# Last steps of a down-projection taken bank by bank, one weight cast with a narrower wait, the last bank in two halves, and a new order of the final normalisation

## The chip, the cores and the metric

The kernel runs on one core of one Trainium2 chip. The metric is device time in microseconds, the median over runs; the kernel before takes 1745.13 us (three runs, 1744.98 to 1745.54).

## What is computed

One decoder layer over 256 tokens with 2048 features, in float32. The part that matters here is its last block, a gated feed-forward layer with a residual and a normalisation behind it:

```python
h = rmsnorm(x, g_pre_ffn[l])
up = causal_dwconv(h @ w_up[l], w_fconv[l], b_fconv[l])
gate, val = jnp.split(up, 2, axis=-1)
x = x + rmsnorm((jax.nn.gelu(gate, approximate=True) * val) @ w_down[l], g_post_ffn[l])
```

`w_up` is 2048 x 11264 and `w_down` 5632 x 2048. `rmsnorm(y, g)` is `y * rsqrt(mean(y*y) + 1e-6) * g` over the 2048 features of a token.

## The kernel before

**Split products.** Each float32 factor is held as a high part (rounded for the matrix unit, type fp32r) and a low part (what the rounding left). A product takes three matmuls, high x high, low x high and high x low (`TERMS`, `rows_mm`, line 540 for its matmul).

**Weight pieces.** All weights come as pieces of up to 1 MB through four slots. For each piece SyncE's queue loads `raw[slot]` once `lo_done` says that the slot's former piece is split (`piece`, L359); ScalarE rounds it into `wsp[slot, 0]` (`hi`, the cast, L1004, semaphore `hi_done`); VectorE subtracts for the low part (`lo`, L1437, `lo_done`); TensorE waits with `arrive` for `lo_done`. A cast may overwrite a slot only when TensorE is done with the piece in it. TensorE counts `gemm_step` for that, and a `Phase` says how many steps a piece is behind: `ph.g(i, 0)` is the count at which trip i begins, `ph.used[c]` the steps of a trip after which piece c is no longer needed. The cast is issued two pieces ahead (`LEAD`), so in a trip of four pieces `hi` is called with c = 2, 3 (the slots 2 and 3 of this trip) and 4, 5 (slots 0 and 1 of the next). For c = 4, 5 it waits for that slot alone; for c = 2, 3 it waits for `ph.g(i, 0)`, that is for all four pieces of the trip before.

**Feed-forward.** The 44 hidden blocks of 128 features go in three groups of 16, 16 and 12 (`GROUPS`). In each, the up-projection (`up_round`) makes the hidden rows in `hsp`, and then the down-projection adds them up in all eight PSUM banks `ps`: bank 4m + b holds tokens 128m to 128m + 127 and output columns 512b to 512b + 511. One weight piece is one hidden block k: 12 matmuls of 512 columns for m = 1, 12 for m = 0, each 3 to a bank. A trip is four blocks; the groups have 4, 4 and 3 trips. The last trip of a group goes in another order (lines 962 to 982): first m = 0 for its four blocks k, all four banks for each; then m = 1. In the groups 0 and 1, m = 1 is also taken block by block; in group 2 bank by bank, with 12 matmuls to a bank. `dn_done` counts finished banks. VectorE takes the sums to `y_tok` (`dn_y`, L2011 copies in group 0, L2013 adds in the others, semaphore `y_out`), the banks of m = 0 before it splits the next two pieces.

On ScalarE the casts of the down-projection of the groups 0 and 1 stand in a hardware loop over all trips, where the trip number i is a register; in group 2 the last trip is written out apart (`last_apart`), with i a Python number:

```python
rounds(act, dn, dn_round, last_apart=(n == len(GROUPS) - 1))
```

**The end.** After the last split VectorE runs, for each half m of the tokens: `dn_y` for four banks, `gain` (y times the gain row, L2031), `fin_rms` (sum of squares from ScalarE, L2037 to L2038, the square root on ScalarE, L991, and a Newton step of five small operations, L1458 to L1462) and `fin` (scale and residual, L2045). Their order is written out: all `dn_y(0, b)`, all `gain(0, b)`, `fin_rms(0)`, then `dn_y(1, b)`, `fin(0, b)`, `gain(1, b)` for each b, `fin_rms(1)`, and four `fin(1, b)`. ScalarE squares each bank with a running sum (L1421). SyncE loads the gain row into `raw` slot 2 after the last split (L453) and stores each finished quarter of 512 columns, 256 KB (L458).

Of the kernel before, what the change touches and what calls it, by code (L numbers as in the profile page):

```python
# [27 lines left out]
ALU = mybir.AluOpType  # L28
ACT = mybir.ActivationFunctionType
AX = mybir.AxisListType.X  # L30
# [127 lines left out]
def build(nc, a, out):  # L158
# [13 lines left out]
    with ExitStack() as ctx:  # L172
# [3 lines left out]
        def sem(name):  # L176
            return ctx.enter_context(nc.semaphore(name))
# [26 lines left out]
        x3_tok, y_tok = a_tok, b_tok  # L204
        g_row, sq_junk = raw[:, 2, :], raw[:, 3, :]
        yg = scr[:, :].rearrange("p (m d) -> p m d", m=2)

# [69 lines left out]
        dn_done, y_out, g_in = sem("dn_done"), sem("y_out"), sem("g_in")  # L277
        fin_sq, fin_out = sem("fin_sq"), sem("fin_out")

# [72 lines left out]
        def _(sp):  # L352
# [100 lines left out]
            sp.dma_start(g_row, a["g_post_ffn"].to_broadcast([P, D])).then_inc(g_in, 16)  # L453
            for m in range(2):
                for b in range(4):
                    sp.wait_ge(fin_out, 4 * m + b + 1)
                    cols = slice(b * 512, (b + 1) * 512)
                    sp.dma_start(out_tok[:, m, cols], out_sb[:, m, cols]).then_inc(out_stored, 16)  # L458
            sp.wait_ge(out_stored, 128)


        @block.tensor
        def _(pe):
# [454 lines left out]
            for n, ((f0, fn), up, dn) in enumerate(zip(GROUPS, PH_UP, PH_DN)):  # L918
# [43 lines left out]
                i, last_ks = dn.trips - 1, range(fn - 4, fn)  # L962
                for c, k in enumerate(last_ks):
                    arrive(dn, i, c)
                    pe.wait_ge(hid_lo, f0 + k + 1)
                    for b in range(4):
                        mm = dn_mm(c, k, 0, b, False, c == 3)
                        if c == 3:
                            mm.then_inc(dn_done, 1)
                if n < len(GROUPS) - 1:  # L970
                    for c, k in enumerate(last_ks):
                        for b in range(4):
                            mm = dn_mm(c, k, 1, b, False, c == 3)
                            if c == 3 and b < 3:
                                mm.then_inc(dn_done, 1)
                        mm.then_inc(gemm_step, 1)
                else:
                    for b in range(4):
                        for c, k in enumerate(last_ks):
                            mm = dn_mm(c, k, 1, b, False, c == 3)  # L980
                        mm.then_inc(dn_done, 1)


        @block.scalar
        def _(act):
# [7 lines left out]
            def hi(ph, i, c):  # L993
# [4 lines left out]
                if c >= SLOTS and c - SLOTS < ph.n:  # L998
                    act.wait_ge(gemm_step, ph.g(i, ph.used[c - SLOTS]))
                elif not isinstance(i, int) or ph.g(i, 0) > 0:  # L1000
                    act.wait_ge(gemm_step, ph.g(i, 0))
# [415 lines left out]
            act.wait_ge(lo_done, PIECES)  # L1417
            for m in range(2):
                for b in range(4):
                    act.wait_ge(y_out, 8 * (len(GROUPS) - 1) + 4 * m + b + 1)  # L1420
                    act.activation(sq_junk[:, b * 512:(b + 1) * 512], y_tok[:, m, b * 512:(b + 1) * 512], ACT.Square,  # L1421
                                   accum_out=st[:, 40 + 4 * m + b:41 + 4 * m + b]).then_inc(fin_sq, 1)
                root(9 + m, st[:, 4 + m:5 + m], st[:, 2 + m:3 + m])


        @block.vector
        def _(dve):
# [598 lines left out]

            def gain(m, b):

                cols = slice(b * 512, (b + 1) * 512)
                dve.wait_ge(y_out, 8 * (len(GROUPS) - 1) + 4 * m + b + 1)  # L2030
                own.mark(dve.tensor_tensor(yg[:, m, cols], y_tok[:, m, cols], g_row[:, cols], ALU.mult))  # L2031

            def fin_rms(m):

                v, root_, r0, r = (st[:, at + m:at + m + 1] for at in (2, 4, 6, 26))
                dve.wait_ge(fin_sq, 4 * m + 4)
                own.link(dve.tensor_reduce(st[:, 48 + m:49 + m], st[:, 40 + 4 * m:44 + 4 * m], AX, ALU.add))  # L2037
                dve.tensor_scalar(v, st[:, 48 + m:49 + m], 1.0 / D, EPS, ALU.mult, ALU.add).then_inc(var_ready, 1)  # L2038
                dve.wait_ge(root_ready, 9 + m)
                newton(v, root_, r0, r)  # L2040

            def fin(m, b):

                cols = slice(b * 512, (b + 1) * 512)
                dve.scalar_tensor_tensor(out=out_sb[:, m, cols], in0=yg[:, m, cols], scalar=st[:, 26 + m:27 + m],  # L2045
                                         in1=x3_tok[:, m, cols], op0=ALU.mult, op1=ALU.add).then_inc(fin_out, 1)
            dve.wait_ge(lo_done, PIECES)
            for b in range(4):
                dn_y(0, b)
            dve.wait_ge(g_in, 16)  # L2050
            for b in range(4):
                gain(0, b)
            fin_rms(0)
            own.wait()
            for b in range(4):
                dn_y(1, b)
                fin(0, b)
                gain(1, b)
            fin_rms(1)
            own.wait()  # L2060
            for b in range(4):
                fin(1, b)

# [107 lines left out]
```

## Time and profile before

| | |
|---|---|
| median of three runs | 1745.13 us |
| the profiled execution's own time | 1745.46 us |
| its span, first to last instruction | 1743.6 us |
| TensorE busy, share of the span | 1727.1 us, 99% |
| VectorE, ScalarE, GpSimd busy | 1141.3, 913.1, 157.1 us |
| mean granted TensorE clock | 0.997 |

The profiled execution lies 1.86 us above its span (launch and end, outside the first and last instruction) and 0.33 us above the median of the runs. Times in the rows further down are microseconds from the span's start; PE is TensorE, PEld its weight loads, DVE VectorE, ACT ScalarE, SPq the issue of transfers by SyncE. A matmul's busy time overlaps the next one's start, so a rate is read from the starts: the stretch between two starts divided by the number of matmuls.

### The profile page before, as it was taken

To read this page: it belongs to the slowest core of one execution; us is meant where nothing else is said; L and a number is where in the kernel's file an instruction comes from. 1 tells how busy PE (TensorE), PEld (TensorE's weight loads), DVE (VectorE), ACT (ScalarE), POOL (GpSimd) and SP (SyncE) were. 2 spreads that over 40 slices of the span, in tenths; PEclk is the share of its full clock that TensorE was granted. 3 is DMA by queue.
4 is the path that set the end of the run, shared out by engine and by line. 5 is a ranking of instruction groups with operands and counts; after the bars stand their busy time and mean duration, and the time that the engine had idled before them with its cause. 6 is when DMAs were issued, how large, how long until landed. Compare 5 with 4: busy or idle time off the path is not lost.

```text
span 1743.6 us, 25292 instructions
## 1 busy us (share of the span) xinstructions
PE 1727.1 (99%) x8956; PEld 1472.3 (84%) x8956; DVE 1141.3 (65%) x1433; ACT 913.1 (52%) x1160; POOL 157.1 (9%) x182
## 2 busy tenths in 40 slices
PE   8999999999999999999999999999999999999997
PEld 7888888888888888888888888888888888888886
DVE  6766675467788874446567677775467776467765
ACT  6656654454567763344447565554345555245542
POOL 0012210000244430000000000000000000000000
PEclk9999999999999999999999999999999999999999
DMA  9544457566555665555654455556465556545552
GB/s 328 191 128 151 155 179 249 193 241 193 171 184 165 196 218 193 193 193 199 235 193 170 145 173 182 180 188 236 150 193 187 181 182 235 180 152 185 192 221 93
DMA packets 214091, 330.09 MB, mean 189 GB/s; under 512 B 5904, under 2 KB 161936, under 8 KB 206608
## 3 DMA queue, kind: packets, MB, share of 16 engines
q1 hardware_dynamic: 208400, 318.49, 54.3%
q10 hardware_dynamic: 5632, 10.79, 1.8%
q8 instruction: 40, 0.66, 0.2%
q14 instruction: 19, 0.16, 0.0%
HBM read 327.16 MB, written 2.10 MB: 189 GB/s over the span
## 4 chain that ended last, share of the span: by engine, by line
PE 98%; DVE 1%; DMA 0%; ACT 0%; SPq 0%; issue 0%; DVEq 0%; ACTq 0%
PE ps L492 50%; PE ps L540 40%; PE ps L508 2%; PE ps L602 1%; PE ps L752 1%; PE ps L680 1%; DMA raw<-in_w_in 0%; PE ps L572 0%; PE ps L709 0%; PE ps L685 0%; PE ps L702 0%; DVE wsp L1437 0%; PE ps L710 0%; PE ps L840 0%; PE ps L824 0%; ACT wsp L1004 0%
## 5 line engine op out<-in xcount | busy, mean ns | idle before, releaser
L1437 DVE TENSOR_TENSOR wsp<-raw,wsp 128x2048 fp32r<-128x2048 f32 (+2 forms) x306 | 676.5, 2230 | 339.7 <-ACT wsp L1004 336.4
L1004 ACT ACTIVATE wsp<-raw 128x2048 fp32r<-128x2048 f32 (+2 forms) x306 | 559.9, 1850 | 297.5 <-PE ps L540 282.2
L492 PE MATMUL ps<-asp,wsp 128*128 128x512 f32 (+1 forms) x3072 | 543.5, 339 | 2.1 <-DVE big_a L1445 1.4
L492 PEld LDWEIGHTS ps<-asp,wsp 128*128 128x128 f32 x3072 | 470.9, 188 | 72.6 <-DVE wsp L1437 1.7
L540 PE MATMUL ps<-wsp,hsp 128*128 128x512 f32 x2304 | 525.7, 389 | 0.0
L540 PEld LDWEIGHTS ps<-wsp,hsp 128*128 128x128 f32 x2304 | 432.1, 188 | 89.5
L492 PE MATMUL ps<-hsp,wsp 128*128 128x256 f32 (+1 forms) x1944 | 353.6, 341 | 3.1 <-DVE hsp L1481 3.1
L492 PEld LDWEIGHTS ps<-hsp,wsp 128*128 128x128 f32 x1944 | 299.9, 189 | 47.2 <-DVE wsp L1437 3.5
L540 PE MATMUL ps<-wsp,asp 128*128 128x512 f32 x768 | 175.5, 389 | 0.0
L1015 ACT ACTIVATE cr<-ps 128x256 f32<-128x256 f32 x185 | 69.0, 379 | 197.7 <-PE ps L492 181.4
L540 PEld LDWEIGHTS ps<-wsp,asp 128*128 128x128 f32 x768 | 143.9, 188 | 29.8
L2133 POOL TENSOR_TENSOR scr<-scr 128x256 f32<-128x256 f32 x44 | 34.1, 795 | 1004.7 <-DVE scr L1963 1004.7
L1378 ACT ACTIVATE scr<-scr,par 128x256 f32<-128x256 f32 x88 | 48.2, 595 | 60.7 <-DVE scr L1952 60.7
L1445 DVE TENSOR_TENSOR cr<-ps,cr 128x256 f32<-128x256 f32 x88 | 35.1, 419 | 44.7 <-ACT cr L1015 44.7
L1957 DVE SCALAR_TENSOR_TENSOR scr<-scr,par 128x255 f32<-128x255 f32 x88 | 42.5, 484 | 27.4 <-ACT scr L1378 27.2
L2114 POOL TENSOR_TENSOR scr<-scr 128x256 f32<-128x256 f32 x16 | 28.5, 1781 | 246.9 <-ACT scr L1190 246.9
L508 PE MATMUL ps<-wsp,asp 128*128 128x512 f32 (+1 forms) x256 | 47.4, 340 | 0.0
L1404 ACT ACTIVATE hsp<-scr 128x256 f32 (+1 forms) x44 | 18.4, 418 | 53.3 <-POOL scr L2133 53.3
L508 PEld LDWEIGHTS ps<-wsp,asp 128*128 128x128 f32 x256 | 40.0, 188 | 5.8
L1992 DVE TENSOR_TENSOR hsp<-scr,hsp 128x256 f32 (+1 forms) x44 | 18.8, 427 | 36.1 <-ACT hsp L1404 36.1
L1109 ACT ACTIVATE scr<-scr,st 128x128 f32<-128x128 f32 (+1 forms) x32 | 14.3, 448 | 49.2 <-DVE st L1615 49.2
L1963 DVE SCALAR_TENSOR_TENSOR scr<-scr,par 128x254 f32<-128x254 f32 x88 | 38.4, 478 | 0.0
(227 smaller groups left out, 910.1 us busy)
## 6 DMA issues: line engine op xcount, KB each, us to landing
raw<-in_w_up SPq DMA_DIRECT2D x88, 1024.0 KB, 5.3
raw<-in_w_in SPq DMA_DIRECT2D x64, 1024.0 KB, 5.4
raw<-in_w_down SPq DMA_DIRECT2D x44, 1024.0 KB, 5.2
raw<-in_w_in SPq DMA_DIRECT2D x32, 768.0 KB, 4.4
raw<-in_w_o_mla SPq DMA_DIRECT2D x16, 1024.0 KB, 5.3
raw<-in_w_o_lru SPq DMA_DIRECT2D x16, 1024.0 KB, 5.1
raw<-in_w_out SPq DMA_DIRECT2D x16, 1024.0 KB, 5.0
raw<-in_w_ukv SPq DMA_DIRECT2D x8, 1024.0 KB, 5.4
```

What stands on the lines that cost most here:

```text
L492: mm = pe.matmul(ps[:, bank, 0:w], lhs(part, k), x[:, 0:w], start=(f and part == 0), stop=(l and n == 1))
L508: mm = pe.matmul(o, x, r, start=(f and part == 0), stop=(l and n == 1))
L540: mm = pe.matmul(ps[:, bank, :], src[:, k, low * T + m * P:low * T + (m + 1) * P], wsp[:, c, part, cols], start=(first and t == 0), stop=( ...
L1004: act.activation(wsp[:, p0 % SLOTS, 0, 0:n], raw[:, p0 % SLOTS, 0:n], ACT.Copy).then_inc(hi_done, 1)
L1015: act.activation(cr[:, slot, :], ps[:, bank, T:2 * T], ACT.Copy, scale=scale).then_inc(cross_done, 1)
L1378: act.activation(UC[2 * v + e], UR[2 * v + e], ACT.Identity, scale=col(W_F + 2 * P, m), bias=col(B_F, m)).then_inc(up_bias, 1)
L1437: dve.tensor_tensor(wsp[:, slot, 1, 0:n], raw[:, slot, 0:n], wsp[:, slot, 0, 0:n].bitcast(F32), ALU.subtract).then_inc(lo_done, 1)
L1445: return dve.tensor_tensor(dst, ps[:, bank, 0:T], cr[:, slot, :], ALU.add)
L1957: own.mark(dve.scalar_tensor_tensor(out=buf[:, 1:T], in0=src[:, 0:T - 1], scalar=col(W_F + P, m), in1=buf[:, 1:T], op0=ALU.mult, op1=ALU.add))
L1963: dve.scalar_tensor_tensor(out=buf[:, 2:T], in0=src[:, 0:T - 2], scalar=col(W_F, m), in1=buf[:, 2:T], op0=ALU.mult, op1=ALU.add).then_inc( ...
L2114: own.mark(pool.tensor_tensor(IG[e], IG[e], XC[e], ALU.mult))
L2133: pool.tensor_tensor(HID[e], UC[e], UC[2 + e], ALU.mult).then_inc(hid_out, 1)
```

## The change

1. In the last trip of **every** group, the m = 0 part now takes its first two blocks as before, and the last two together: for each bank, three matmuls of the third block and three of the fourth. TensorE therefore waits for the fourth piece before the first matmul of the third.
2. `hi` gets a branch: where i is a Python number above 0 and the phase has four pieces a trip, the casts with c = 2, 3 wait for their own slot in the trip before.
3. In group 2, m = 1: banks 0 to 2 as before; the last bank's 12 matmuls of 512 columns become 24 of 256, in two halves. The first half goes on in bank 7; the second starts afresh in bank 0, and VectorE adds both what bank 7 held for these columns and bank 0.
4. The final normalisation is reordered: VectorE waits for the gain row before its first `dn_y`; `dn_y` and `gain` alternate; the finishing operations of m = 0 are spread between the sums of m = 1; the Newton step has three operations in place of five; ScalarE loads its square-root table ahead; the last root takes one addend by `bias`. For m = 1, quarter 0 is finished by TensorE (identity times residual, plus diag(scale) times y*gain, both in plain float32), copied by ScalarE and stored through ScalarE's queue; quarters 1, 2 and the halves of 3 by VectorE and SyncE's queue.

```diff
@@ sync
+            for b in range(4):
+                store(0, quarter(b), b + 1)
+            store(1, quarter(1), 5)
+            store(1, quarter(2), 6)
+            for h in range(2):
+                store(1, LAST[h], 7 + h)
@@ tensor
-                for c, k in enumerate(last_ks):
-                    arrive(dn, i, c)
-                    pe.wait_ge(hid_lo, f0 + k + 1)
+                for cs in ((0,), (1,), (2, 3)):
+                    for c in cs:
+                        arrive(dn, i, c)
+                        pe.wait_ge(hid_lo, f0 + last_ks[c] + 1)
                     for b in range(4):
-                        mm = dn_mm(c, k, 0, b, False, c == 3)
+                        for c in cs:
+                            mm = dn_mm(c, last_ks[c], 0, b, False, c == 3)
...
-                    for b in range(4):
+                    for b in range(3):
                         for c, k in enumerate(last_ks):
                             mm = dn_mm(c, k, 1, b, False, c == 3)
                         mm.then_inc(dn_done, 1)
+                    for h in range(2):
+                        if h:
+                            pe.wait_ge(y_out, 8 * n + 1)
+                        for c, k in enumerate(last_ks):
+                            for t, (part, low) in enumerate(TERMS):
+                                mm = pe.matmul(ps[:, 0 if h else 7, 0:T], hsp[:, k, low * T + P:low * T + 2 * P], wsp[:, c, part, LAST[h]],
+                                               start=(h == 1 and c == 0 and t == 0), stop=(c == 3 and t == 2))
+                        mm.then_inc(dn_done, 1)
+                    pe.wait_ge(y_out, 8 * n + 2)
+                    pe.matmul(ps[:, 1, :], ident[:, :], x3_tok[:, 1, quarter(0)], start=True, stop=False)
+                    pe.wait_ge(y_gain, 1)
+                    pe.wait_ge(fin_diag, 1)
+                    pe.matmul(ps[:, 1, :], diag[0], yg[:, 1, quarter(0)], start=False, stop=True).then_inc(fin_mm, 1)
@@ scalar, hi
                     act.wait_ge(gemm_step, ph.g(i, ph.used[c - SLOTS]))
+                elif isinstance(i, int) and i and ph.n == SLOTS:
+                    act.wait_ge(gemm_step, ph.g(i - 1, ph.used[c]))
                 elif not isinstance(i, int) or ph.g(i, 0) > 0:
                     act.wait_ge(gemm_step, ph.g(i, 0))
@@ scalar, the end
+            act.activation(diag[0], ident[:, :], ACT.Copy, scale=st[:, 27:28]).then_inc(fin_diag, 1)
+            act.wait_ge(fin_mm, 1)
+            act.activation(out_sb[:, 1, quarter(0)], ps[:, 1, :], ACT.Copy).then_inc(fin_first, 1)
+            act.wait_ge(fin_first, 1)
+            act.dma_start(out_tok[:, 1, quarter(0)], out_sb[:, 1, quarter(0)]).then_inc(out_stored, 16)
@@ vector, the end
             dve.wait_ge(lo_done, PIECES)
+            dve.wait_ge(g_in, 16)
             for b in range(4):
                 dn_y(0, b)
-            dve.wait_ge(g_in, 16)
-            for b in range(4):
                 gain(0, b)
...
+            fin(0, quarter(0))
+            dn_y(1, 0)
+            gain(1, 0, y_gain)
+            fin(0, quarter(1))
+            dn_y(1, 1)
+            gain(1, 1)
+            fin(0, quarter(2))
+            fin(0, quarter(3))
+            dn_y(1, 2)
+            gain(1, 2)
```

**TensorE, end of the down-projection of group 1.** A row is an instruction in issue order, xN how many like it follow one another; each pair of a waiting row and an x11 row is one block of m = 0, and the rows shown begin with the third block before, the second block after. Before:

```order
L540 MATMUL ps<-wsp,hsp 128x512 [waits hid_lo,lo_done]
L540 MATMUL ps<-wsp,hsp 128x512 x11
L540 MATMUL ps<-wsp,hsp 128x512 [waits hid_lo,lo_done]
L540 MATMUL ps<-wsp,hsp 128x512 x59
L345 UNCONDITIONAL_BRANCH [waits y_out]
```

After:

```order
L547 MATMUL ps<-wsp,hsp 128x512 [waits hid_lo,lo_done]
L547 MATMUL ps<-wsp,hsp 128x512 x11
L547 MATMUL ps<-wsp,hsp 128x512 [waits lo_done,hid_lo]
L547 MATMUL ps<-wsp,hsp 128x512 x71
L347 UNCONDITIONAL_BRANCH [waits y_out]
```

The wait for the fourth piece has moved up by 12 matmuls, to the head of the third block. The groups 0 and 2 show the same.

**VectorE, from the last two splits on, after the change.** (`big_b` is `y_tok`, `scr` holds y*gain, `raw` the output; before, the first four L2056 stood together and the four L2074 behind them.)

```order
L1480 TENSOR_TENSOR wsp<-raw,wsp 128x2048 [waits hi_done] x2
L2056 TENSOR_TENSOR big_b<-big_b,ps 128x512 [waits dn_done,g_in,lo_done]
L2074 TENSOR_TENSOR scr<-big_b,raw 128x512 [waits y_out]
L2056 TENSOR_TENSOR big_b<-big_b,ps 128x512 [waits dn_done]
L2074 TENSOR_TENSOR scr<-big_b,raw 128x512 [waits y_out]
```

The first sum now waits for the transfer of the gain row, and each `gain` follows the `dn_y` that it needs.

```order
L2088 SCALAR_TENSOR_TENSOR raw<-scr,st,big_a 128x512 x2
L2056 TENSOR_TENSOR big_b<-big_b,ps 128x512 [waits dn_done]
L2074 TENSOR_TENSOR scr<-big_b,raw 128x512 [waits y_out]
L2118 TENSOR_TENSOR big_b<-big_b,ps 128x256 [waits dn_done]
L2119 TENSOR_TENSOR big_b<-big_b,ps 128x256
L2121 TENSOR_REDUCE st<-st 128x1 [waits fin_sq]
L2122 TENSOR_SCALAR st<-st 128x1 [waits dve_self]
L2124 TENSOR_TENSOR big_b<-big_b,ps 128x256 [waits dn_done,dve_self]
```

Two finishing operations of m = 0 (L2088) now stand ahead of the sum of bank 6 and of the last bank; the last bank takes three sums of 256 columns in place of one of 512.

## Rows read from the trace of the kernel before

**Rows 1.** The page: span, busy us, share of it and instruction count by engine.

```profile
span 1743.6 us, 25292 instructions
...
PE 1727.1 (99%) x8956; PEld 1472.3 (84%) x8956; DVE 1141.3 (65%) x1433; ACT 913.1 (52%) x1160; POOL 157.1 (9%) x182
```

**Rows 2.** Who waited for whom on TensorE: total us, times, longest.

```profile
PE ps L492 <- DVE hsp L1481: 3.1, 1, 3.1
...
PE ps L492 <- DVE big_a L1445: 1.4, 1, 1.4
```

**Rows 3.** Timeline of TensorE, group 0's down-projection (start us, length us, instruction, count).

```profile
1179.66 87.21 PE L540 MATMUL ps<-wsp,hsp 128*128 128x512 f32 x384
1266.71 0.50 PE L492 MATMUL ps<-asp,wsp 128*128 128x512 f32 x2
```

**Rows 4.** Timeline of group 0's last trip: casts and splits.

```profile
1245.23 3.72 ACT L1004 ACTIVATE wsp<-raw 128x2048 fp32r<-128x2048 f32 x2 [9.04 <-PE ps L540]
1247.18 4.49 DVE L1437 TENSOR_TENSOR wsp<-raw,wsp 128x2048 fp32r<-128x2048 f32 x2 [8.67 <-ACT wsp L1004]
```

**Rows 5.** Timeline, TensorE, group 1's down-projection.

```profile
1446.86 87.21 PE L540 MATMUL ps<-wsp,hsp 128*128 128x512 f32 x384
1533.91 0.85 PE L492 MATMUL ps<-asp,wsp 128*128 128x512 f32 x4
```

**Rows 6.** Timeline of group 1's last trip: its last two splits.

```profile
1514.38 4.50 DVE L1437 TENSOR_TENSOR wsp<-raw,wsp 128x2048 fp32r<-128x2048 f32 x2 [8.67 <-ACT wsp L1004]
```

**Rows 7.** Timeline around 82 us, TensorE released by VectorE: one VectorE row.

```profile
82.35 0.42 DVE L1445 TENSOR_TENSOR big_a<-ps,cr 128x256 f32<-128x256 f32 x1
```

**Rows 8.** Timeline, TensorE's first matmul after that wait.

```profile
82.91 0.47 PE L492 MATMUL ps<-asp,wsp 128*128 128x512 f32 x1 [1.42 <-DVE big_a L1445]
```

**Rows 9.** Timeline, TensorE, group 2's down-projection.

```profile
1669.02 65.44 PE L540 MATMUL ps<-wsp,hsp 128*128 128x512 f32 x288
```

**Rows 10.** Timeline of the end, from the casts of the last trip on.

```profile
1712.75 3.72 ACT L1004 ACTIVATE wsp<-raw 128x2048 fp32r<-128x2048 f32 x2 [8.96 <-PE ps L540]
1714.69 4.49 DVE L1437 TENSOR_TENSOR wsp<-raw,wsp 128x2048 fp32r<-128x2048 f32 x2 [8.59 <-ACT wsp L1004]
1719.21 0.34 SPq L453 DMA_DIRECT2D raw<-in_g_post_ffn  x1
1721.66 2.66 DVE L2013 TENSOR_TENSOR big_b<-big_b,ps 128x512 f32<-128x512 f32 x4 [2.47 <-PE ps L540]
...
1728.22 0.69 DVE L2013 TENSOR_TENSOR big_b<-big_b,ps 128x512 f32<-128x512 f32 x1
1728.82 0.75 DVE L2045 SCALAR_TENSOR_TENSOR raw<-scr,st,big_a 128x512 f32<-128x512 f32 x1
...
1734.51 0.69 DVE L2013 TENSOR_TENSOR big_b<-big_b,ps 128x512 f32<-128x512 f32 x1 [0.61 <-PE ps L540]
...
1735.23 0.63 ACT L1421 ACTIVATE raw<-big_b 128x512 f32<-128x512 f32 x1 [1.84 <-DVE big_b L2013]
...
1737.95 2.74 DVE L2045 SCALAR_TENSOR_TENSOR raw<-scr,st,big_a 128x512 f32<-128x512 f32 x4
```

**Rows 11.** Timeline of TensorE: 512 and 256 columns in turn; plain float32.

```profile
473.84 1.89 PE L752 MATMUL ps<-scr,cur 128*128 128x256 f32 x8
475.38 22.82 PE L492 MATMUL ps<-hsp,wsp 128*128 128x512 f32 x128
498.04 0.38 PE L752 MATMUL ps<-scr,cur 128*128 128x256 f32 x1
```

**Rows 12.** Windows after the last matmul: granted clock, DMA share, GB/s.

```profile
1734.50:1738.50 4.00, 0.00 (x0) 1.00 0.26 98
1739.50:1742.50 3.00, 0.00 (x0) 0.50 0.99 348
```

**Rows 13.** Transfers at the end: count, KB each, median us to landing.

```profile
out<-raw SPq DMA_DIRECT2D x8, 256.0 KB, 2.4
raw<-in_g_post_ffn SPq DMA_DIRECT2D x1, 1024.0 KB, 4.9
```

More of the change, by code:

```diff
@@ L205, in build @@
         g_row, sq_junk = raw[:, 2, :], raw[:, 3, :]
+        LAST = [slice(D - 512 + h * T, D - 512 + (h + 1) * T) for h in range(2)]
         yg = scr[:, :].rearrange("p (m d) -> p m d", m=2)
@@ L453, in _, with store @@
             sp.dma_start(g_row, a["g_post_ffn"].to_broadcast([P, D])).then_inc(g_in, 16)
[L454 to L459 removed]
+            def store(m, cols, count):
+                sp.wait_ge(fin_out, count)
+                sp.dma_start(out_tok[:, m, cols], out_sb[:, m, cols]).then_inc(out_stored, 16)
+            for b in range(4):
[4 more added lines that the diff above has]
+                store(1, LAST[h], 7 + h)
+            sp.wait_ge(out_stored, 16 * 9)
         @block.tensor
@@ L2025, in _, with gain @@
                         dn_y(1, b)
-            def gain(m, b):
-                cols = slice(b * 512, (b + 1) * 512)
+            def gain(m, b, done=None):
+                cols = quarter(b)
                 dve.wait_ge(y_out, 8 * (len(GROUPS) - 1) + 4 * m + b + 1)
[L2031 to L2040, printed above, removed]
@@ L2052, in _ @@
                 gain(0, b)
-            fin_rms(0)
-            own.wait()
[L2055 to L2062, printed above, removed]
+            dve.wait_ge(fin_sq, 4)
+            own.link(dve.tensor_reduce(c1(50), st[:, 40:44], AX, ALU.add))
+            dve.tensor_scalar(c1(2), c1(50), 1.0 / D, EPS, ALU.mult, ALU.add).then_inc(var_ready, 1)
@@ new lines, in _ @@
+            y0, n_dn = 8 * (len(GROUPS) - 1), 7 * (len(GROUPS) - 1)
+            dve.wait_ge(dn_done, n_dn + 8)
+            y = [y_tok[:, 1, LAST[h]] for h in range(2)]
+            dve.tensor_tensor(y[0], y[0], ps[:, 7, 0:T], ALU.add).then_inc(y_half, 1)
+            own.mark(dve.tensor_tensor(y[1], y[1], ps[:, 7, T:2 * T], ALU.add))
+            dve.wait_ge(fin_sq, 7)
+            own.link(dve.tensor_reduce(c1(50), st[:, 44:47], AX, ALU.add))
+            own.link(dve.tensor_scalar(c1(50), c1(50), 1.0 / D, EPS, ALU.mult, ALU.add))
@@ new lines, in _ @@
+            dve.wait_ge(dn_done, n_dn + 9)
+            dve.tensor_tensor(y[1], y[1], ps[:, 0, 0:T], ALU.add).then_inc(y_half, 1)
+            dve.wait_ge(fin_sq, 8)
+            dve.scalar_tensor_tensor(out=c1(51), in0=c1(47), scalar=1.0 / D, in1=c1(50), op0=ALU.mult, op1=ALU.add).then_inc(var_ready, 1)
+            dve.wait_ge(y_half, 2)
+            own.mark(dve.tensor_tensor(yg[:, 1, quarter(3)], y_tok[:, 1, quarter(3)], g_row[:, quarter(3)], ALU.mult))
+            dve.wait_ge(var_ready, 10)
@@ new lines, in _ @@
+            own.link(dve.tensor_scalar(c1(53), c1(51), -0.5, None, ALU.mult))
+            dve.wait_ge(fin_sq, 9)
+            own.link(dve.scalar_tensor_tensor(out=c1(53), in0=c1(48), scalar=-0.5 / D, in1=c1(53), op0=ALU.mult, op1=ALU.add))
+            dve.wait_ge(root_ready, 10)
+            scale_rows(c1(53), c1(5), c1(7), c1(9), c1(27)).then_inc(fin_scale, 1)
+            dve.wait_ge(fin_scale, 1)
+            own.wait()
+            fin(1, quarter(1))
+            fin(1, quarter(2))
+            for h in range(2):
+                fin(1, LAST[h])
```

46 lines of the change are left out of this document (36 added, 10 removed).

## The prediction

> **What bounds the kernel now.** I read the page first: TensorE is busy 1727.1 of 1743.6 us [rows 1]. Then who waited for whom on TensorE: five waits, none in the feed-forward layer or behind it; the longest and the one that matters below stand in [rows 2]. So there TensorE is fed without a gap, and any wait that the change gives it there is paid in full: nothing behind it has slack to give back. Third, the timeline of TensorE over the down-projections: 384 matmuls of 512 columns from 1179.66 to 1266.71 us, so 0.2267 us each [rows 3]. Fourth, the timeline of the end: behind TensorE's last matmul some 9 us are left, in which VectorE and then the stores set the pace [rows 10, 12]. The change touches both: a wait in all three groups, and the end.
>
> **Part 1, the third and fourth block of m = 0 together.** The matmuls are the same in number and shape, so they cost nothing; what moves is the wait for the fourth piece, 12 matmuls (2.7 us) ahead. Whether it is ready then is read group by group.
>
> Group 0: the last 72 matmuls (24 of m = 0, 48 of m = 1) end where the next phase starts, 1266.71, so the third block starts at 1266.71 - 72 x 0.2267 = 1250.39. Both casts of the last trip are issued together once the trip before is done (1245.23, two in 3.72 us), and the two splits end at 1247.18 + 4.49 = 1251.67 [rows 3, 4]. Today the fourth block starts at 1253.11, 1.44 us behind that end; now it would be wanted 1.28 us ahead of it. A matmul that VectorE releases starts 0.14 us behind VectorE's end (82.35 + 0.42 to 82.91), and the one after it comes some 0.08 us late, since its weight load isn't hidden [rows 7, 8] (the 0.08 is my reading of that restart). TensorE stalls 1.28 + 0.14 + 0.08 = 1.5 us.
>
> Group 1: the third block starts at 1533.91 - 16.32 = 1517.59, the splits end at 1514.38 + 4.50 = 1518.88 [rows 5, 6]. 1.29 + 0.22 = 1.5 us again.
>
> Part 2 of the change, the narrower wait of the cast, doesn't help here: it asks for i as a Python number above 0, and in the groups 0 and 1 the casts stand in a hardware loop, where i is a register. It helps in group 2 alone. There the last trip starts at 1669.02 + 192 x 0.2267 = 1712.54 [rows 9]. The third cast now goes when its own slot is free, one block (5.4 us) earlier, so the fourth is first in line at 1712.75, takes 1.9, and its split (4.49 / 2 = 2.25) ends near 1717.0 [rows 10]. The third block starts at 1712.54 + 5.44 = 1717.98. No stall, by 1 us; without the narrower wait it would have been 1.4 us. The other places where i is such a number (KV up-projection, output projection, last trips of Q and LRU) gain nothing, since TensorE doesn't wait for a cast in any of them [rows 2]; the 1.4 us wait at 82 us is for VectorE's sum of a tile, and there the cast stands in ScalarE's order behind copies that wait for the whole trip anyway.
>
> **Sum of the steady part: 2 x 1.5 = +3.0 us.** Bounds: 0, if the fourth piece were ready in time after all; and 2 x 1.7, if the restart took twice what [rows 7, 8] give.
>
> **Part 3, the last bank in halves.** In the stretch of 512 and 256 columns in turn, 128 matmuls take 22.66 us (475.38 to 498.04) [rows 11]; taking 64 x 0.2267 off leaves 0.127 us for one of 256. 24 of them take 3.05 us where 12 of 512 took 2.72, so TensorE ends 0.3 us later, near 1734.8. The same row shows that a weight load in front of each 256-column matmul is hidden. (What it would cost if it weren't is the fourth rival.) The Trainium skill, in "TensorE: Matmul & The Clock Gate", under "The mechanism", says that a weight load overlaps running matmuls only when it goes to another row group, and under "LDWEIGHTS" that it takes its columns over 1.2 ns, 107 ns here. By that rule each half-width matmul would take 107 + 107 ns, 24 of them 5.1 us, and TensorE would end 2.4 us later instead of 0.3; the trace speaks against it.
>
> **Part 4, the end.** Is TensorE or VectorE late? VectorE's walk, with spacings from [rows 10]: a sum of 512 columns occupies it 0.60 (1728.22 to 1728.82), a gain as much, a finishing operation 0.66 (four in 2.74); where the next one needs the result it is 0.69 + 0.03. A scale (reduce, root, Newton) is 1737.95 - 1734.51 - 0.60 - 0.66 - 0.60 = 1.58, of eight steps, 0.2 each; two fewer now, 1.2.
> - Start: the last split ends near 1717.0 instead of 1719.2, and the gain row is issued then; it lands 4.9 later [rows 13], 1721.9. VectorE now waits for it ahead of the first sum: 1721.9 against 1721.66.
> - Four sums each followed by its own gain: 4 x (0.72 + 0.60) = 5.3, to 1727.2.
> - Scale of m = 0: 0.15 for the last square, 1.2: 1728.55. Before, it was done at 1728.2.
> - Four finishing operations, three sums and three gains: 4 x 0.66 + 3 x 1.32 = 6.6, to 1735.15. Before, VectorE had only three of the finishing operations ahead of the last bank and idled 0.61 us for it.
> - So it is now VectorE that is late: TensorE has the first half ready near 1733.3 and the second near 1734.8. Two sums of 256 (0.33 each), reduce and add (0.4), third sum (0.42): 1736.6. Gain 0.6, five small operations 0.95, the root on ScalarE beside them: first finishing operation of m = 1 at about 1738.25, against 1737.95.
> - Stores: from 1739.5 to 1742.5 the transfer engines are 99% busy at 348 GB/s [rows 12]: four quarters, 1 MB, are 3.0 us of transfer. Taking one quarter off VectorE shortens its work from 2.74 to 2.2 us, but the same 1 MB leaves from the time that the first quarter is ready. So the end moves with the first finishing operation, by +0.3.
>
> The quarter that TensorE now finishes: scale ready 1738.25, diagonal on ScalarE some 0.4, one plain float32 matmul of 512 columns 0.86 (four of 256 took 1.54 plus the overlap, 0.43 each [rows 11]), a copy 0.63: stored from about 1740.3, as VectorE's last one. It decides nothing if the clock is full, and it is for 4.0 us after the last matmul at least [rows 12]; the identity matmul moves that a us on.
>
> **Sum of the end: +0.3 us,** between -1.2 (VectorE never behind: sum 0.42, square 0.5, root 0.2, three small 0.6 and 0.3 of TensorE's in place of 3.44) and +0.8.
>
> **Total: 3.0 + 0.3 = +3.3 us.** The profiled execution (1745.46) would take 1748.8; against the median of 1745.13, 1748.4. A measurement of this kernel can tell about 0.2%, 3.5 us, from no change; the forecast is just inside.
>
> **Rivals.**
> - *The end pays as it is meant to.* VectorE's backlog is smaller than I walked it, the scale of m = 1 hangs on TensorE again, and the end gives 1.2 us: 3.0 - 1.2, 1746.9. For: the new order of small operations is shorter behind the last sum. Against: the walk leaves 1.9 us between the first half's readiness and VectorE. Chance 0.15.
> - *No stall.* TensorE gets the fourth piece in time, because the casts of the groups 0 and 1 go earlier than I read; then only the end counts, -1.2 to +0.3: 1744.5, on the faster side. It decides if the splits end before 1250.2. Against: the loop's casts still wait for the whole trip, and the splits end 1.3 us too late. Chance 0.05.
> - *The quarter on TensorE comes last.* Its store leaves through ScalarE's queue behind four others. If the granted clock has fallen to half, as in [rows 12] from 1739.5 on, its matmul takes 1.7 instead of 0.86, the copy ends near 1741.2, and with 2.5 us to landing the end is at 1743.7 instead of 1743.24 + 0.3: total +3.0 + 0.6 or more, 1748.9. It decides once the quarter is issued later than 1741.0.  Chance 0.10.
> - *Weight loads aren't hidden in a run of 256-column matmuls.* Each would pay its load, 1472.3 us / 8956 = 0.16 [rows 1], on top of 0.127: 24 x 0.29 = 7.0 us, the second half ready near 1738.8 instead of 1736.2, when VectorE wants it: +2.6, 1751.0. It decides once a matmul takes over 0.18 us. Against: 0.127 in [rows 11], though between 512-column ones. This is what the skill's rule on row groups would make of it. Chance 0.03.
> - *The narrower wait doesn't do its work in group 2*: a third stall of 1.4 us, the gain row 2.2 us later, total +6.5, 1751.6. Chance 0.03.
>
> **Numbers.** Forecast (both stalls, VectorE behind): 0.64, at 1748.4, give or take 0.7. The range 1746.4 to 1749.5 holds it, the first rival and most of the third. Slower by over 0.2% (above 1748.6): 0.24 of the forecast's 0.64, and the third, fourth and fifth rival: 0.40. Faster by over 0.2%: 0.02. The same: 0.58.
>
> **What the profile after would show.** TensorE idle twice, 1.3 to 1.6 us, released by VectorE's L1480, near 1250 and 1519, and the next up-projections starting at 1268.2 and 1536.9; group 2 without one. The third cast of the last trip near 1710 by the clock shifted by 3 us. At the end VectorE without idle time from its first sum to the first sum of the last bank, that one well behind TensorE. I am wrong if TensorE's count of waits doesn't grow, or if the stretch from the last matmul to the end shrinks by over a us.

## The result, and the profile after

The changed kernel takes 1748.87 us (median of 12 runs, 1747.94 to 1750.0), the kernel before beside it 1745.18 (12 runs, 1744.66 to 1746.15): ratio 1.0022, 95% interval 1.0014 to 1.0029, or +3.7 us. The forecast was 1748.4, in a range of 1746.4 to 1749.5. The time lies within it, 0.5 above the forecast. The median is just over the bound of 0.2% that I had given 0.40, against 0.58 for "the same"; since the interval has that bound inside it, which side the kernel is on isn't decided. The profiled execution took 1748.52.

The page after, beside [rows 1]:

```profile
span 1746.7 us, 25334 instructions
...
PE 1728.8 (99%) x8972; PEld 1473.3 (84%) x8972; DVE 1142.0 (65%) x1435; ACT 915.7 (52%) x1165; POOL 157.1 (9%) x182
```

Who waited for whom on TensorE, after, beside [rows 2]: one new entry in the down-projection (two waits, line 547), and one at the very end that costs nothing by itself (line 1003, the diagonal product). A third new entry, 0.9 us of issue at line 637, lies near 50 us, before the stretches compared below.

```profile
PE ps L1003 <- ACT mask L1462: 3.2, 1, 3.2
...
PE ps L547 <- DVE wsp L1480: 2.8, 2, 1.4
...
PE ps L499 <- DVE big_a L1488: 1.4, 1, 1.4
```

The timeline of TensorE over the down-projections of groups 0 and 1, beside [rows 3, 5]. What was one row of 384 matmuls is now 312 and 72, with 1.38 us of idle time between, in both groups:

```profile
1179.33 70.88 PE L547 MATMUL ps<-wsp,hsp 128*128 128x512 f32 x312
1251.59 16.59 PE L547 MATMUL ps<-wsp,hsp 128*128 128x512 f32 x72 [1.38 <-DVE wsp L1480]
1268.02 7.21 PE L499 MATMUL ps<-asp,wsp 128*128 128x512 f32 x40
```

```profile
1448.17 70.89 PE L547 MATMUL ps<-wsp,hsp 128*128 128x512 f32 x312
1520.44 16.60 PE L547 MATMUL ps<-wsp,hsp 128*128 128x512 f32 x72 [1.38 <-DVE wsp L1480]
1536.88 23.37 PE L499 MATMUL ps<-asp,wsp 128*128 128x512 f32 x132
```

Group 0's last trip, beside [rows 4]: casts and splits stand where they stood (0.34 us earlier, the whole execution is), and TensorE now waits for their end, 1246.84 + 4.49 = 1251.33. Behind it the four banks are finished 1.36 us apart (six matmuls each), and VectorE waits 0.67 us for each of the last three; that costs nothing here, as the run with the narrower cast wait shows further down.

```profile
1244.89 3.72 ACT L1028 ACTIVATE wsp<-raw 128x2048 fp32r<-128x2048 f32 x2 [9.04 <-PE ps L547]
1246.84 4.49 DVE L1480 TENSOR_TENSOR wsp<-raw,wsp 128x2048 fp32r<-128x2048 f32 x2 [8.67 <-ACT wsp L1028]
...
1253.26 0.69 DVE L2054 COPY big_b<-ps 128x512 f32<-128x512 f32 x1 [1.92 <-PE ps L547]
1254.62 0.69 DVE L2054 COPY big_b<-ps 128x512 f32<-128x512 f32 x1 [0.67 <-PE ps L547]
```

The end, beside [rows 9, 10, 11]. First TensorE, then the other engines (ACTq is the issue of a transfer by ScalarE):

```profile
1671.99 62.73 PE L547 MATMUL ps<-wsp,hsp 128*128 128x512 f32 x276
1734.56 3.04 PE L996 MATMUL ps<-wsp,hsp 128*128 128x256 f32 x24
1737.43 1.02 PE L1000 MATMUL ps<-big_a,ident 128*128 128x512 f32 x2
1741.64 1.10 PE L1003 MATMUL ps<-scr,mask 128*128 128x512 f32 x2 [3.19 <-ACT mask L1462]
```

```profile
1710.28 1.92 ACT L1028 ACTIVATE wsp<-raw 128x2048 fp32r<-128x2048 f32 x1 [3.52 <-PE ps L547]
...
1715.72 1.92 ACT L1028 ACTIVATE wsp<-raw 128x2048 fp32r<-128x2048 f32 x1 [3.52 <-PE ps L547]
...
1717.67 2.29 DVE L1480 TENSOR_TENSOR wsp<-raw,wsp 128x2048 fp32r<-128x2048 f32 x1 [3.15 <-ACT wsp L1028]
1719.99 0.34 SPq L455 DMA_DIRECT2D raw<-in_g_post_ffn  x1
...
1724.65 0.69 DVE L2056 TENSOR_TENSOR big_b<-big_b,ps 128x512 f32<-128x512 f32 x1 [4.69 <-DMA raw<-in_g_post_ffn]
...
1731.35 0.75 DVE L2088 SCALAR_TENSOR_TENSOR raw<-scr,st,big_a 128x512 f32<-128x512 f32 x1
...
1737.98 0.41 DVE L2118 TENSOR_TENSOR big_b<-big_b,ps 128x256 f32<-128x256 f32 x1
...
1739.01 0.42 DVE L2124 TENSOR_TENSOR big_b<-big_b,ps 128x256 f32<-128x256 f32 x1
...
1741.10 2.21 DVE L2088 SCALAR_TENSOR_TENSOR raw<-scr,st,big_a 128x512 f32<-128x512 f32 x4
...
1743.40 0.39 ACTq L1466 DMA_DIRECT2D out<-raw  x1
```

The third cast of group 2 comes early (1710.28, its own slot only), the fourth at 1715.72, and TensorE doesn't stall: 276 matmuls in one row. VectorE's first sum starts at 1724.65, released by the gain row, and from there no row of VectorE shows a wait for another engine up to the finishing operations at 1741.10; it takes up the first half of the last bank at 1737.98, which TensorE had done near 1736.3 (an estimate: 1734.56 + 12 x 0.12, and 0.28 for the record of one such matmul).

**Two stretches take the noise out.** Across the traces of all runs, group 0's down-projection starts anywhere between 1178.5 and 1180.4 us. The spread arises early: TensorE's first long wait, near 16 us, took 2.39 us in the trace with the earliest start (pairs only, 1178.51) and 3.82 in the one with the latest (1180.38, without the narrow wait). A spread of the runs of 1 to 2 us is thus to be expected, whatever the edit. Two differences within a trace are free of it: from the start of group 0's to the start of group 2's down-projection ("steady"), and from there to the end of the span ("end"). Starts are TensorE's rows such as the ones above, spans the pages', which have one decimal: an "end" is good to 0.05 us, a difference of two to 0.1. The last column is how long the two records of the diagonal product took, as TensorE's timeline gives it.

| kernel | median, before beside it | steady | end | diagonal product |
|---|---|---|---|---|
| before | 1745.18 | 489.36 | 74.58 | |
| changed | 1748.87, 1745.18 | 492.66 | 74.71 | 1.10 |
| groups 0, 1 unpaired | 1745.86, 1744.92 | 489.36 | 74.93 | 2.02 |
| narrow cast wait in all groups | 1745.24, 1744.92 | 489.36 | 75.24 | 2.04 |
| gain row early | 1747.22, 1744.92 | 492.69 | 73.67 | 1.94 |
| both mends | 1743.77, 1744.92 | 489.36 | 73.38 | 1.10 |
| pairs only, on before | 1750.27, 1745.07 | 492.67 | 76.22 | |
| changed, no narrow wait | 1751.66, 1745.07 | 492.70 | 77.02 | 1.10 |
| both mends, quarter 0 by VectorE | 1744.36, 1745.07 | 489.36 | 73.70 | |
| both mends, clock kept | 1744.38, 1745.07 | 489.36 | 73.41 | 1.10 |
| both mends again | 1744.01, 1745.18 | 489.36 | 73.42 | 1.10 |
| both mends, no pairs | 1746.14, 1745.18 | 489.36 | 75.06 | 2.04 |
| before, gain row early | 1745.46, 1745.18 | 489.36 | 74.60 | |
| both mends, last bank whole | 1744.42, 1745.18 | 489.36 | 74.20 | 2.05 |

So the change costs 3.3 us in the steady part and 0.1 at the end, 3.4 of the 3.7 that the medians show. The other 0.3 isn't located; it is within what the start moves.

### The profile page after: what moved, and what is told of

It is laid out like the page before. It is cut to its first block, busy times and chain, and to the rows that moved or that the text cites. A ratio compares the mean times of both kernels' runs of the same rounds, so it can differ in the third digit from the quotient of the medians.

```text
span 1746.7 us, 25334 instructions
## 1 busy us (share of the span) xinstructions
PE 1728.8 (99%) x8972; PEld 1473.3 (84%) x8972; DVE 1142.0 (65%) x1435; ACT 915.7 (52%) x1165; POOL 157.1 (9%) x182
## 4 chain that ended last, share of the span: by engine, by line
PE 96%; DVE 2%; ACT 1%; DMA 1%; issue 0%; SPq 0%; ACTq 0%; DVEq 0%
PE ps L499 50%; PE ps L547 38%; PE ps L515 2%; PE ps L609 1%; DVE wsp L1480 1%; PE ps L759 1%; PE ps L687 1%; ACT wsp L1028 1%; DMA raw<-in_w_in 0%; PE ps L579 0%; PE ps L716 0%; PE ps L692 0%; PE ps L709 0%; DMA raw<-in_g_post_ffn 0%; DVE big_b L2056 0%
```

## The experiments

My theory was: two stalls of TensorE are the loss, the end is a draw because VectorE is late from the gain row on. The rivals: the end costs, or pairing costs by itself.

**Groups 0 and 1 unpaired** (the changed kernel, pairs in group 2 only).

```diff
-                for cs in ((0,), (1,), (2, 3)):
+                for cs in (((0,), (1,), (2, 3)) if n == len(GROUPS) - 1 else ((0,), (1,), (2,), (3,))):
```

> The changed kernel, but groups 0 and 1 take the four blocks of m = 0 one after the other, as before; group 2 and the end stay changed. If the two stalls of TensorE (1.38 us of idle time each in the trace after, 1.6 with the restart) are the cost, this is 3.3 us faster than the changed kernel and 0.2 to 0.5 us slower than the kernel before, and TensorE's list of waits has no entry on the down-projection. If it is the end that costs (rival), it stays 2 us or more slower than the kernel before.

Measured 1745.86 us, ratio to before 1.0004 (0.9995 to 1.0013): 0.9 above the kernel before, where the changed kernel is 3.7 above, so 2.8 are back. The steady part is at 489.36 again, to the hundredth. The 0.9 is more than I expected; the clock at the end is part of it (below).

**The narrow cast wait in all groups.** This keeps the pairs and mends their cause: with the last trip of the casts written out, i is a number in every group.

```diff
-                rounds(act, dn, dn_round, last_apart=(n == len(GROUPS) - 1))
+                rounds(act, dn, dn_round, last_apart=True)
```

> The changed kernel, with the last trip of the casts written out apart in all three groups, so that the narrower wait also applies to groups 0 and 1; the pairs of blocks stay. If the late fourth piece is the cause, both stalls go and the time is that of the run with groups 0 and 1 unpaired, within 0.4 us: 3.3 us faster than the changed kernel. If pairing itself costs (six matmuls on one bank in a row, or earlier evictions meeting other work), 1 us or more of the loss stays.

Measured 1745.24 us, ratio 1.0002 (0.9993 to 1.0011), 0.3 above the kernel before: 3.4 us of the 3.7 are back. TensorE's rows are whole again in both groups:

```profile
1178.80 87.21 PE L547 MATMUL ps<-wsp,hsp 128*128 128x512 f32 x384
1265.85 9.34 PE L499 MATMUL ps<-asp,wsp 128*128 128x512 f32 x52
```

The steady part is at 489.36 with the pairs in place. So the pairs cost nothing by themselves; the late fourth piece was the whole of the steady part's 3.3 us.

**Gain row early.** Its slot, `raw` 2, is free when the third piece is split.

```diff
-            sp.wait_ge(lo_done, PIECES)
+            sp.wait_ge(lo_done, PIECES - 1)
             sp.dma_start(g_row, a["g_post_ffn"].to_broadcast([P, D])).then_inc(g_in, 16)
```

> The changed kernel, with the gain row's load waiting only for the split of the third last-trip piece, whose slot it takes, instead of the fourth: issued 5.4 us earlier. If VectorE's walk from the row's landing on is what sets the end, the first sum starts when bank 0 is done (about 2 us earlier), VectorE waits for the last half again, and the time falls by 1.3 us against the changed kernel. If the store transfers or TensorE's last half set the end, it falls by less than 0.3.

Measured 1747.22 us, ratio 1.0013 (1.0004 to 1.0022): 2.3 above the kernel before instead of 3.7, so 1.4 for the mend; by the trace's end stretch 74.71 - 73.67 = 1.04, with the clock at half here, and 1.3 with it full (both mends, next). The timeline shows the chain that was expected: the row issued at 1713.78, the first sum released by TensorE rather than by a transfer, and VectorE waiting 0.51 us for the second half of the last bank (line 2124), where in the changed kernel it was VectorE that came late. Counted from group 2's start, the finishing operations begin 67.79 us in (1739.02 - 1671.23) against 69.11 (1741.10 - 1671.99) in the changed kernel: 1.32 earlier, a measure that the clock of the last product doesn't touch.

```profile
1713.78 0.34 SPq L455 DMA_DIRECT2D raw<-in_g_post_ffn  x1
...
1721.85 0.69 DVE L2056 TENSOR_TENSOR big_b<-big_b,ps 128x512 f32<-128x512 f32 x1 [2.66 <-PE ps L547]
...
1736.94 0.42 DVE L2124 TENSOR_TENSOR big_b<-big_b,ps 128x256 f32<-128x256 f32 x1 [0.51 <-PE ps L996]
...
1739.02 2.21 DVE L2088 SCALAR_TENSOR_TENSOR raw<-scr,st,big_a 128x512 f32<-128x512 f32 x4
```

**Both mends.**

> The changed kernel with both: narrower wait of the cast in all groups, and the early gain row. The two effects lie in different stretches and should add: 3.3 + 1.3 = 4.6 us faster than the changed kernel, 0.9 us faster than the kernel before. If the end is bound by something else, it only equals the kernel before within 0.4.

Measured 1743.77 us, ratio to before 0.9993 (0.9984 to 1.0002), and in the repetition further down 1744.01, ratio 0.9992 (0.9983 to 1.0001): 1.15 and 1.17 us under the kernel before. The effects add: from 3.7 above to 1.15 below is 4.8, against 3.3 + 1.3 = 4.6 by the stretches. Each interval just includes 1, so by the runs alone it is a likely gain and not a sure one; the two traces say the same twice, an end of 73.38 and 73.42 against 74.58. VectorE's first sum and its first finishing operation of m = 1:

```profile
1718.64 0.69 DVE L2056 TENSOR_TENSOR big_b<-big_b,ps 128x512 f32<-128x512 f32 x1 [2.66 <-PE ps L547]
...
1735.82 2.21 DVE L2088 SCALAR_TENSOR_TENSOR raw<-scr,st,big_a 128x512 f32<-128x512 f32 x4
```

**Pairs only, on the kernel before** (the loop of the diff over `cs`, nothing else).

> The kernel before with one edit: the third and fourth block of m = 0 taken together in all three groups, and no narrower wait. If the late fourth piece is the cause, TensorE stalls three times by 1.6 us, once in each group, also in group 2 where the old end stays: 3 x 1.6 = 4.9 us slower than the kernel before. If the two stalls of the changed kernel had another cause (its other edits), it is within 1 us of the kernel before.

Measured 1750.27 us, ratio 1.0030 (1.0019 to 1.0041), +5.2; by the stretches 3.31 + 1.64 = 4.95. Three stalls, one in each group:

```profile
PE ps L540 <- DVE wsp L1439: 4.1, 3, 1.4
```

```profile
1671.18 49.12 PE L540 MATMUL ps<-wsp,hsp 128*128 128x512 f32 x216
1721.60 16.60 PE L540 MATMUL ps<-wsp,hsp 128*128 128x512 f32 x72 [1.30 <-DVE wsp L1439]
```

Pairing alone makes the loss, with none of the other edits.

**The changed kernel without the narrow wait.**

```diff
-                elif isinstance(i, int) and i and ph.n == SLOTS:
-                    act.wait_ge(gemm_step, ph.g(i - 1, ph.used[c]))
```

> The changed kernel without the new branch of the cast. Group 2 stalls as well, by 1.6 us, and the last split and with it the gain row come 2.2 us later. If VectorE's walk from the gain row sets the end, TensorE's stall is hidden under it and the time rises by 2.2 us against the changed kernel; if the stall sets it, by 1.6; if both are paid one after the other (as the last rival of the prediction had it, 1751.6 in all), by about 3.

Measured 1751.66 us, ratio 1.0036 (1.0022 to 1.0049), 6.6 above the kernel before instead of 3.7, so 2.9 by medians, and 2.31 by the end stretch (77.02 against 74.71). The three prices were 2.2, 1.6 and about 3. The medians are nearest to the third, and the time itself is the prediction's 1751.6 for the last rival; but they rest on five runs here, and the start moves by more than the 0.8 between the first price and the third. The trace speaks for the first: the first sum comes 54.96 us into group 2 (1728.04 - 1673.08) against 52.66 in the changed kernel, 2.30 later, and the whole end is 2.31 longer. So TensorE's third stall (1.30 us idle) hides under VectorE's walk, which starts when the gain row has landed. It is one profile against a median that doesn't bear it out, so the price is likely 2.3 and not settled by the runs.

```profile
1673.08 49.12 PE L547 MATMUL ps<-wsp,hsp 128*128 128x512 f32 x216
1723.51 13.88 PE L547 MATMUL ps<-wsp,hsp 128*128 128x512 f32 x60 [1.30 <-DVE wsp L1478]
```

```profile
1723.28 0.34 SPq L455 DMA_DIRECT2D raw<-in_g_post_ffn  x1
...
1728.04 0.69 DVE L2054 TENSOR_TENSOR big_b<-big_b,ps 128x512 f32<-128x512 f32 x1 [4.79 <-DMA raw<-in_g_post_ffn]
```

**Quarter 0 by VectorE**, on both mends: the two products, the diagonal, the copy and ScalarE's store are out, and `fin(1, quarter(0))` with its store stands ahead of quarter 1.

```diff
-                    pe.matmul(ps[:, 1, :], ident[:, :], x3_tok[:, 1, quarter(0)], start=True, stop=False)
...
-                    pe.matmul(ps[:, 1, :], diag[0], yg[:, 1, quarter(0)], start=False, stop=True).then_inc(fin_mm, 1)
...
+            fin(1, quarter(0))
             fin(1, quarter(1))
```

> The kernel with both mends, but quarter 0 of m = 1 is finished by VectorE ahead of quarter 1 and stored by SyncE, with no identity or diagonal matmul and no copy. If the stores' 3 us of transfer set the end, the median stays within 0.3 us of the kernel with both mends, and it spreads less from run to run, since it no longer hangs on TensorE's clock. If VectorE's finishing operations set it, it is 0.6 us slower. If the half-clock matmul (1.9 to 2.0 us for the two records in three of the five traces so far, 1.1 in the others) costs in most runs, it is 0.3 us or more faster.

Measured 1744.36 us, ratio 0.9995 (0.9986 to 1.0004). The end stretch is 73.70, 0.3 longer than with TensorE's help at full clock and the same as with it at half clock (73.67). So to finish quarter 0 on TensorE is worth 0.3 us at full clock and nothing at half; the medians, 0.44 apart against the kernel before, can't tell this from the expected "within 0.3" or 0.6. The spread of the runs, 1.6 us, is no smaller than with both mends (1.3 and 1.5), so the clock of that product isn't the main thing that spreads them.

**Clock kept**, on both mends.

```diff
+                    pe.wait_ge(y_out, 8 * n + 3)
+                    for _ in range(7):
+                        pe.matmul(ps[:, 2, 0:P], ident[:, :], ident[:, :], start=True, stop=True)
                     pe.wait_ge(y_gain, 1)
```

> The kernel with both mends, and seven matmuls of identity times identity (128 columns, 1.5 us in all) into the unused bank 2 between the identity and the diagonal product, so that TensorE is busy up to the diagonal product. If the fall of the clock before that product costs, the product takes 1.1 us in every profile, and the median is 0.2 to 0.5 us lower than with both mends. If the product isn't on the path, nothing changes within 0.2.

Measured 1744.38 us, ratio 0.9996 (0.9987 to 1.0005). The product took 1.10, and the end stretch of 73.41 is that of both mends with full clock. The median is 0.7 under the kernel before where both mends are 1.15, so it shows none of the gain of 0.2 to 0.5 that a clock kept up would have given, and the difference between the two is too small to call a loss; the one profile can't tell how often the clock would have fallen.

**Both mends again**, as the measure for the two variants of it below.

> The kernel with both mends once more, as the measure for the two variants of it in this group. Expected 1.1 us faster than the kernel before, as in its first comparison; the stretch from the first matmul of group 2's down-projection to the end of the span was 73.4 us with the full clock at the diagonal product, and 73.7 where the clock had fallen.

Measured 1744.01 us, end stretch 73.42.

**Both mends, no pairs.**

```diff
-                for cs in ((0,), (1,), (2, 3)):
+                for cs in ((0,), (1,), (2,), (3,)):
```

> The kernel with both mends, and the four blocks of m = 0 one after the other in every group, as before. Bank 0 of group 2 is then done 2.0 us later (39 matmuls into the trip instead of 30). If VectorE's walk from its first sum on sets the end, the stretch from group 2's first matmul to the end grows by about 1.3 to 2.0 us against both mends; if TensorE's last half sets it, by less than 0.3.

Measured 1746.14 us, ratio to before 1.0004 (0.9995 to 1.0013), 2.1 above both mends. The end stretch is 75.06, 1.39 above the 73.67 that the same end took with the pairs and the clock also at half (the run with the gain row early). Counted to the finishing operations, free of the clock, it is 1.3: 69.11 us into group 2 (1737.85 - 1668.74) against 67.80 (1735.82 - 1668.02). VectorE's first sum starts at 1721.40 with group 2 starting at 1668.74, 52.66 us in, against 50.62 (1718.64 - 1668.02) with pairs.

```profile
1721.40 0.69 DVE L2056 TENSOR_TENSOR big_b<-big_b,ps 128x512 f32<-128x512 f32 x1 [4.70 <-PE ps L547]
```

```profile
1668.74 62.73 PE L547 MATMUL ps<-wsp,hsp 128*128 128x512 f32 x276
...
1738.40 2.04 PE L1003 MATMUL ps<-scr,mask 128*128 128x512 f32 x2 [3.20 <-ACT mask L1462]
```

So the pairs are worth 1.3 to 1.4 us in group 2, once the gain row is early. In the changed kernel they can have been worth nothing: its first sum waited for the row until 52.66 us in, and without pairs bank 0 is ready at just that point. This follows from the two starts; no run takes the pairs out of the changed kernel's group 2.

**Before, with the early gain row.** (The same one-line edit as above.)

> The kernel before with one edit: the gain row is loaded after the third split of the last trip instead of after the fourth. There both splits come together, so the load is issued 2.2 us earlier, and VectorE does its four sums first, which end at 1724.3 in the trace of before, when the row had landed. No change within 0.3 us, which says that the early row helps only with the new order, where the first sum waits for it.

Measured 1745.46 us, ratio 0.9999 (0.9990 to 1.0008), end stretch 74.60 against 74.58: nothing, as expected. The early row mends something that the new order of the sums had made.

**Both mends, last bank whole.**

```diff
-                    for b in range(3):
+                    for b in range(4):
...
-            own.mark(dve.tensor_tensor(y[1], y[1], ps[:, 7, T:2 * T], ALU.add))
+            dve.tensor_tensor(y[1], y[1], ps[:, 7, T:2 * T], ALU.add).then_inc(y_half, 1)
...
-            dve.tensor_tensor(y[1], y[1], ps[:, 0, 0:T], ALU.add).then_inc(y_half, 1)
```

> The kernel with both mends, and the last bank in one piece of 12 matmuls with 512 columns (VectorE adds it in two parts of 256 and the squares stay in halves). TensorE is done with it 0.3 us earlier than with the second half, but 1.2 later than with the first. VectorE comes to the first half only when it is just ready, so I expect the end 0.1 to 0.4 us later than with both mends; if the halves are worth what they cut off (the bank's 2.7 us halved), 1.2 us later.

Measured 1744.42 us, against 1744.01 for both mends again. The finishing operations start at 1736.65 with group 2 at 1668.40, 68.25 us in, against 67.80 (1735.82 - 1668.02) with halves: the halves give 0.45 us, a little above my 0.1 to 0.4, and far from 1.2. (The end stretch, 74.20, is 0.8 longer, but its diagonal product ran at half clock.)

```profile
1736.65 2.21 DVE L2080 SCALAR_TENSOR_TENSOR raw<-scr,st,big_a 128x512 f32<-128x512 f32 x4
```

```profile
1668.40 65.45 PE L547 MATMUL ps<-wsp,hsp 128*128 128x512 f32 x288
...
1737.20 2.05 PE L995 MATMUL ps<-scr,mask 128*128 128x512 f32 x2 [2.49 <-ACT mask L1454]
```

## Why the prediction was right, step by step

- **Two stalls, right in place, count and cause.** The third block of groups 0 and 1 waits for a fourth piece that is cast only when the whole trip before is done; mending the cast alone removes it, pairing alone makes it. The size was 0.15 us short for each: forecast 1.5, measured 1.65 (492.66 - 489.36 = 3.30 for two). The term that was mis-sized is the release: I took 0.14 us from VectorE's end to TensorE's matmul, from [rows 7, 8], and it took 0.26 here (1251.33 to 1251.59). The lateness was right (the third block wanted at 1179.33 + 312 x 0.2267 = 1250.06, so 1.27 where I had 1.28), and the restart took 0.11 (72 matmuls from 1251.59 end at 1267.91, the next starts at 1268.02) where I had 0.08; that it is a weight load which isn't hidden stays my reading. Where [rows 8] follow a wait for one event, here the third block waits for both pieces and for hidden rows; that the further waits cost the difference is argued, not shown.
- **No stall in group 2, right.** Split's end at 1717.67 + 2.29 = 1719.96, the paired blocks wanted from 1671.99 + 216 x 0.2267 = 1720.96: a margin of 1.0 us, as forecast. Without the narrower wait a stall appears with 1.30 us of idle time and, with release and restart, 1.6 in all (1.64 by the end stretch of pairs only), where I had 1.4.
- **The last bank in halves, right.** From 1734.56 to 1737.43, 24 matmuls take 0.120 us each, where I took 0.127, so TensorE ends 0.15 us later, not 0.3. The rival in which the loads aren't hidden is out: it decided from 0.18 us for a matmul on. This also speaks against the rule in the Trainium skill, "TensorE: Matmul & The Clock Gate", "The mechanism", by which weight loads would overlap only with another row group: with the 107 ns that the same page's "LDWEIGHTS" gives a load, these 24 would by my estimate have taken 5.1 us instead of the measured 2.9. The same section also lets a load go ahead into a background weight buffer, and with that way the 2.9 agree.
- **The end, right to 0.2 us.** Forecast +0.3, measured +0.1 by the stretches. The first sum came 52.66 us into group 2, against 52.64 before (1721.66 - 1669.02), where I had 0.24 later: the gain row took 4.6 us to land, not 4.9. The finishing operations start 69.11 in, against 68.93, so 0.18 later. VectorE was late, as walked, and the early gain row shows that the walk was the bound. That the total fits so well is in part two misses of opposite sign: the stalls 0.3 us too cheap, the end 0.2 too dear.
- **"The end pays as it is meant to"** (0.15) didn't happen here, but was a mend away: 1.3 us of it came with the early row.
- **The quarter on TensorE comes last** (0.10): it happens in some executions. In the three traces with the changed kernel's own end, at full clock the end stretch is 74.71, at half clock 74.93 and 75.24. From the first finishing operation of m = 1 to the end of the span it is 5.6 us in all five traces with the product at full clock and 5.9 to 6.0 in all five with it at half, so the half clock costs 0.3 to 0.4 us. That is the size of what the median's +3.7 has over the profiled pair (3.4), but no run shows that it is that part. The clock fell earlier than I allowed for: I had leaned on 4.0 us at full clock and a us more for the identity product. How often the clock falls in time isn't known from one profile for each kernel, so this share stays open.
- **The last rival's sum was wrong**, though it wasn't the case here: I added the third stall to the later gain row without asking whether they lie beside each other. By the trace they do, with 2.3 us instead of 3.2; the median of that run, 1751.66, is the rival's own figure, which the trace makes a coincidence but the runs alone don't rule out.
- **Slips in the sums.** The walk's own terms give the first finishing operation at 1738.15, not 1738.25 (1736.6 + 0.6 + 0.95). The terms of the lower bound of the end add up to 2.02 in place of 3.44, so -1.4 and not -1.2. The 1743.24 that the third rival starts from stands in no row; the span ends at 1743.6, so that rival's price is uncertain too. None of them moves the forecast out of the range.
- **The chances** leaned to "the same" where the median fell just outside it: 0.58 on within 0.2%, with a forecast 0.2 us from the bound and two stall terms that I had bounded upwards (to 1.7 each) without moving the middle.

## What to carry to other kernels

A wait that moves up by a few matmuls costs what the piece is late, plus release and restart, in every place where the code is shared and nothing else is later still; look for the place whose producer is written differently (here a hardware loop, where the condition on a Python number is silently false). On an engine that works through a list with no pauses, what starts the list (here the landing of a 1 MB row) sets its end, and a bank that another engine hands over sooner gives nothing until that start is moved. And when a whole-kernel median wanders by 2 us from a stretch that the edit doesn't touch, compare stretches within traces: they repeated to 0.04 us here, the ends within the 0.1 us of their rounding.

## What the runs showed of the hardware

- **The clock at the end.** TensorE's granted clock falls to half (1.2 of 2.4 GHz) at a time after its last dense work that differs from run to run, and with it the plain float32 product of 512 columns takes 2.0 us instead of 1.1. Windows of the run with groups 0 and 1 unpaired, and of both mends again (columns: stretch, its length, PE busy and count, granted clock, DMA share, GB/s):

```profile
1737.00:1739.00 2.00, 0.00 (x0) 1.00 0.00 0
1739.00:1740.00 1.00, 0.92 (x1) 0.56 0.00 0
1740.00:1742.00 2.00, 1.11 (x2) 0.50 0.94 328
```

```profile
1737.00:1739.00 2.00, 1.10 (x2) 1.00 0.21 78
1739.00:1740.00 1.00, 0.00 (x0) 1.00 1.03 373
```

  In the first, TensorE finished its identity product at 1736.03 and the clock is at 0.56 in the stretch from 1739; in the second it finished at 1735.63 and is still at full clock when the product comes at 1737.51, and up to 1740. The idle time alone doesn't tell them apart: after the same 1.88 us of idle time the product took 1.94 with the gain row early and 1.10 with both mends, and after 3.19 us in the changed kernel it took 1.10. In the kernel before the clock was full for 4.0 us after the last matmul [rows 12], which I had leaned on.
- **A plain float32 product by itself** takes 1.10 us at full clock, where I had 0.86 from the spacing in [rows 11]. In the changed kernel ScalarE's copy of its result starts 0.03 us behind the record's end (1742.77), so the 1.10 is time that is waited for. That a product which stands alone also shows the end of its pipeline is my reading, not tested.
- **A start of group 0's down-projection that wanders by 1.9 us** from run to run, 1.4 of it in TensorE's first long wait, and steady stretches that agree to 0.01 us (489.36 in ten traces).
